# Up products of a decoder's gated MLPs: 512 columns of both activation parts at once, with the parts summed outside TensorE

## What is computed

```
def _causal_depthwise_conv(u, w, b):      # width 3, per channel
    ...
def _conv_glu_ffn(h, w_up, conv_w, conv_b, w_down):
    u = _causal_depthwise_conv(h @ w_up, conv_w, conv_b)
    gate, val = jnp.split(u, 2, axis=-1)
    return (jax.nn.silu(gate) * val) @ w_down
...
    x = x + gate2 * _conv_glu_ffn(h, ...)   # per layer
...
    return _rms_norm(x, final_gain)
```

## Time and profile before

| | us |
|---|---|
| median of 3 runs | 715.25 (714.64 to 716.34) |
| the profiled execution, its own time | 715.83 |
| span of its trace | 714.1 |
| granted TensorE clock, mean | 0.993 |
| TensorE busy | 692.5 |
| VectorE busy | 500.2 |
| ScalarE busy | 394.6 |
| GpSimd busy | 125.4 |

### The profile page before, as it was taken

The page is one execution under the profiler, slowest core; times in us unless marked ns, Lnnn a source line. Parts: engine busy times, 40 slices in busy tenths (PEclk is TensorE's granted clock), DMA queues, the critical chain, the costliest instruction groups (busy, mean ns, idle before and its releaser), DMA issues.

```text
span 714.1 us, 15023 instructions
## 1 busy us (share of the span) xinstructions
PE 692.5 (97%) x6280; PEld 649.6 (91%) x6280; DVE 500.2 (70%) x901; ACT 394.6 (55%) x633; POOL 125.4 (18%) x96
## 2 busy tenths in 40 slices
PE   7989999999999999999999999999999999999995
PEld 7787888899999999999998888879999999999993
DVE  0564897747888879798657469883786666766666
ACT  2367655734746464646545675673575555444552
POOL 2001004004054555553010010310400000000002
PEclk9999999999999999999999999999999999999998
DMA  8989987565485858587743765656536676555501
GB/s 350 382 256 302 420 297 255 185 229 178 137 314 198 296 179 295 177 293 258 292 153 128 298 246 209 215 200 237 177 117 226 130 247 226 178 177 185 189 40 59
DMA packets 76362, 159.41 MB, mean 223 GB/s; under 512 B 4071, under 2 KB 60168, under 8 KB 67592
## 3 DMA queue, kind: packets, MB, share of 16 engines
q1 hardware_dynamic: 76296, 158.46, 63.4%
HBM read 156.81 MB, written 1.64 MB: 222 GB/s over the span
## 4 chain that ended last, share of the span: by engine, by line
PE 81%; DVE 11%; ACT 4%; issue 2%; DMA 2%; SPq 0%; POOL 0%; DVEq 0%; POOLq 0%
PE bank L961 24%; PE bank L962 23%; PE bank L963 23%; PE bank L974 4%; DVE w_lo L1652 3%; DMA direct<-in_w_ada 2%; ACT work L1543 1%; DVE score L1836 1%; ACT w_hi L1403 1%; PE bank L1007 1%; DVE top L1835 1%; PE bank L1117 1%; PE bank L1222 1%; PE bank L1274 1%; DVE work L1662 1%
## 5 line engine op out<-in xcount | busy, mean ns | idle before, releaser
L961 PE MATMUL bank<-act_hi,w_hi 128*128 128x256 f32 x1040 | 298.3, 287 | 3.4 <-DVE w_lo L1652 3.3
L1652 DVE TENSOR_TENSOR w_lo<-raw,w_hi 128x2048 fp32r<-128x2048 f32 (+1 forms) x97 | 235.4, 2427 | 94.3 <-ACT w_hi L1403 94.1
L962 PE MATMUL bank<-act_lo,w_hi 128*128 128x256 f32 x1040 | 294.9, 284 | 0.0
L963 PE MATMUL bank<-act_hi,w_lo 128*128 128x256 f32 x1040 | 294.8, 283 | 0.0
L1403 ACT ACTIVATE w_hi<-raw 128x2048 fp32r<-128x2048 f32 (+1 forms) x97 | 182.9, 1888 | 140.6 <-PE bank L963 131.3
L961 PEld LDWEIGHTS bank<-act_hi,w_hi 128*128 128x128 f32 x1040 | 200.0, 192 | 7.2 <-issue 4.6
L962 PEld LDWEIGHTS bank<-act_lo,w_hi 128*128 128x128 f32 x1040 | 200.2, 192 | 0.4
L963 PEld LDWEIGHTS bank<-act_hi,w_lo 128*128 128x128 f32 x1040 | 200.1, 192 | 0.0
L1957 DVE SCALAR_TENSOR_TENSOR work<-bank,vec,work 128x254 f32<-128x254 f32 (+1 forms) x176 | 76.5, 476 | 11.1 <-ACT work L1596 9.6
L961 PE MATMUL bank<-mlp_hi,w_hi 128*128 128x256 f32 x192 | 54.7, 285 | 0.0
L962 PE MATMUL bank<-mlp_lo,w_hi 128*128 128x256 f32 x192 | 54.3, 283 | 0.0
(11 more groups left out here) (199 smaller groups left out, 913.0 us busy)
## 6 DMA issues: line engine op xcount, KB each, us to landing
direct<-in_w_ada SPq DMA_DIRECT2D x48, 1024.0 KB, 8.9
raw<-in_w_ffn_up SPq DMA_DIRECT2D x44, 1024.0 KB, 5.2
raw<-in_w_ffn_down SPq DMA_DIRECT2D x22, 1024.0 KB, 5.0
raw<-in_w_in SPq DMA_DIRECT2D x19, 1024.0 KB, 5.2
raw<-in_w_out SPq DMA_DIRECT2D x8, 1024.0 KB, 5.2
raw<-in_w_in SPq DMA_DIRECT2D x2, 984.0 KB, 11.6
bias<-toeplitz SPq DMA_DIRECT2D x4, 384.0 KB, 11.9
xT<-in_x SPq DMA_DIRECT2D x1, 1024.0 KB, 5.0
```

What stands on the lines that cost most here:

```text
L961: pe.matmul(dst, lh, rh, start=first, stop=False, skip_group_check=check)
L962: pe.matmul(dst, lh, rl, start=False, stop=False, skip_group_check=check)
L963: return pe.matmul(dst, ll, rh, start=False, stop=last, skip_group_check=check)
L1652: nc.vector.tensor_tensor(w_lo[n % RAW][:, s], raw[n % RAW][:, s], w_hi[n % RAW][:, s].bitcast(F32), ALU.subtract).then_inc(lo_done, 1)
```

## The change

Both parts of the activations lie side by side for each k (`act_both`). In steps 0 to 9 of both layers, each 128-channel tile of an up unit is now one PSUM tile of 512 columns of its own: per k one product of the high weights with both activation parts (512 columns: high x high in the left half, high x low in the right) and one of the low weights with the high part (256 columns, left half). ScalarE copies the right half to SBUF (`copy_rest`), VectorE adds the left half to it (`sum_tiles`), into `tile_sum`, and the taps read `tile_sum` instead of the bank. Step 10 is as before. The tiles take banks 0, 1, 2 in turn; in step 0 the fourth takes bank 4, in step 1 bank 7. A tile waits for the sum of the tile before it in its bank. Layer 0's last down part moves from bank 2 to bank 6. The second `take_mod` moves to step 0. The end: GpSimd multiplies with the gain only the last part, which ScalarE scales; VectorE scales the three others.

The diff, with unchanged stretches left out (the declarations of new semaphores too):

```
@@ -385,8 +385,8 @@
...
         xT = sb("xT", [P, KT, SEQ])
-        act_hi = sb("act_hi", [P, KT, SEQ], F32R)
-        act_lo = sb("act_lo", [P, KT, SEQ], F32R)
+        act_both = sb("act_both", [P, KT, 2, SEQ], F32R)
+        act_hi, act_lo = act_both[:, :, 0, :], act_both[:, :, 1, :]
         mlp_hi = sb("mlp_hi", [P, 2, SEQ], F32R)
@@ -463,7 +463,8 @@
...
         gate_row, gain_row = v_flat[:, 0:D_MODEL], v_flat[:, D_MODEL:2 * D_MODEL]
-        gained = qkT[:, 2, :, :, :].rearrange("p a b t -> p (a b t)")
+        tile_sum = qkT[:, 0, :, :, :]
+        gained = qkT[:, 2, 0, :, :].rearrange("p b t -> p (b t)")
         squared = [qkT[:, g, half, :, :].rearrange("p b t -> p (b t)") for g in (1, 3) for half in range(2)]
@@ -626,11 +630,23 @@
...
-            return bank[2][:, 0:SEQ] if ct == KT - 1 else bank[3 + ct // 2][:, (ct % 2) * SEQ:(ct % 2 + 1) * SEQ]
+            return bank[3 + ct // 2][:, (ct % 2) * SEQ:(ct % 2 + 1) * SEQ]
...
             return bank[4][:, 0:SEQ] if ct == KT - 1 else bank[ct // 2][:, (ct % 2) * SEQ:(ct % 2 + 1) * SEQ]
+
+        def tile_bank(j, which, f):
+
+            return bank[(0, 1, 2, 7 if j else 4)[2 * which + f] if j < 2 else (4 * j + 2 * which + f - 8) % 3]
+
+        def both_parts(l, j):
+
+            return j < STEPS - 1
+
+        def tiles_of(l):
+
+            return 4 * (STEPS - 1) * l
@@ -822,7 +838,7 @@
...
                 for q in range(2):
-                    sp.wait_ge(out_part[t], q + 1)
+                    sp.wait_ge(out_part[2 * t + q], 1)
                     sp.dma_start(out[0, t * P:(t + 1) * P, 512 * q:512 * q + 512],
@@ -942,15 +958,17 @@
...
                         ada_sum(e[1], e[2])
-            pool.wait_ge(gain_in, 16)
-            for q in range(2):
-                pool.wait_ge(x_out, q + 1)
-                nc.gpsimd.tensor_tensor(gained[:, 512 * q:512 * q + 512], x_tok[:, 0, 512 * q:512 * q + 512],
-                                        gain_row[:, 512 * q:512 * q + 512], ALU.mult).then_inc(row_gained, 1)
-            for t in range(TT):
+            def row_power(t):
+
                 pool.wait_ge(row_ms, t + 1)
...
                     row_root, 1)
+
+            pool.wait_ge(gain_in, 16)
+            row_power(0)
+            pool.wait_ge(x_out, 4)
+            nc.gpsimd.tensor_tensor(gained, x_tok[:, 1, 512:1024], gain_row[:, 512:1024], ALU.mult).then_inc(row_gained, 1)
+            row_power(1)
@@ -1316,15 +1334,43 @@
...
-                def up_first():
-
-                    for which, k0, k1 in [(which, k, k + 1) for k in range(KT // 2) for which in range(2)] + [
-                            (0, KT // 2, KT), (1, KT // 2, KT)]:
-                        mm = unit_product(l, NI + NO + which, bank[which], None if which else KT * (norm + 1), k0, k1)
-                        if k1 == KT:
-                            mm.then_inc(unit_used, 1)
-
-                def up(j, which):
+                def wide_tile(j, which, f, k0, k1, wait_act=None):
+
+
+                    n = unit_no(l, NI + NO + (which if j == 0 else 3 * j - 1 + which))
+                    pe.wait_ge(lo_done, n + 1)
+                    if j:
+                        tile = 4 * j + 2 * which + f
+                        pe.wait_ge(tile_summed, tiles_of(l) + (min(tile, 6) - 3 if tile < 8 else tile - (3 if tile < 11 else 2)))
+                    wh = w_hi[n % RAW][:, :].rearrange("p (k n) -> p k n", k=KT)
+                    wl = w_lo[n % RAW][:, :].rearrange("p (k n) -> p k n", k=KT)
+                    s, dst = slice(f * P, (f + 1) * P), tile_bank(j, which, f)
+                    for k in range(k0, k1):
+                        if wait_act is not None:
+                            pe.wait_ge(act_lo_ready, wait_act + k + 1)
+                        pe.matmul(dst[:, :], wh[:, k, s], act_both[:, k, :, :].rearrange("p a t -> p (a t)"),
+                                  start=k == 0, stop=False, skip_group_check=True)
+                        mm = pe.matmul(dst[:, 0:SEQ], wl[:, k, s], act_hi[:, k, :], start=False, stop=k == KT - 1,
+                                       skip_group_check=True)
+                    if k1 == KT:
+                        mm.then_inc(unit_used if f else first_tile, 1)
+
+                def wide_first():
+
+                    for k in range(KT // 2):
+                        for which in range(2):
+                            for f in range(2):
+                                wide_tile(0, which, f, k, k + 1, None if which or f else KT * (norm + 1))
+                    for which in range(2):
+                        wide_tile(0, which, 0, KT // 2, KT, None if which else KT * (norm + 1))
+                        wide_tile(0, which, 1, KT // 2, KT)
+
+                def wide_up(j, which):
+                    for f in range(2):
+                        wide_tile(j, which, f, 0, KT)
+
+                def single_up(j, which):
+                    pe.wait_ge(tile_summed, tiles_of(l) + 4 * j - 1 + which)
                     pe.wait_ge(conv_read, 2 * (STEPS * l + j - 1) + which + 1)
@@ -1343,8 +1389,8 @@
...
                             mm = product3(down_part(ct), (wh[:, f, s], wl[:, f, s]), (hi[:, f, :], lo[:, f, :]),
-                                          j == 0 and f == 0 and ct in (0, 2, 4, 6, 7), j == STEPS - 1 and f == 1, True)
-                        if j == STEPS - 1 and ct in (1, 3, 5, 6):
+                                          j == 0 and f == 0 and ct % 2 == 0, j == STEPS - 1 and f == 1, True)
+                        if j == STEPS - 1 and ct in (1, 3, 5):
                             mm.then_inc(down_ready, 1)
@@ -1378,13 +1424,17 @@
...
-                down = down_rows if l + 1 == DEPTH else down_product
-                up_first()
+                last = l + 1 == DEPTH
+                down = down_rows if last else down_product
+                wide_first()
                 for j in range(1, STEPS):
+                    up = wide_up if both_parts(l, j) else single_up
                     up(j, 0)
...
                     elif l + 1 == DEPTH and j < 6:
+                        if j == 2:
+                            pe.wait_ge(tile_summed, tiles_of(l) + 8)
                         turn_x(j - 2)
@@ -1588,19 +1638,39 @@
...
                     o = which if j == 0 else 3 * j - 1 + which
-                    act.wait_ge(unit_used, first + o + 1)
+                    if both_parts(l, j):
+                        act.wait_ge(tile_summed, tiles_of(l) + 4 * j + 2 * which + 2)
+                    else:
+                        act.wait_ge(unit_used, first + o + 1)
                     if j > 0:
...
                         ch = which * FT + 2 * j + f
-                        nc.scalar.activation(conv[:, which, f, :], bank[which][:, f * SEQ:(f + 1) * SEQ], ACT.Identity,
+                        src = tile_sum[:, which, f, :] if both_parts(l, j) else bank[which][:, f * SEQ:(f + 1) * SEQ]
+                        nc.scalar.activation(conv[:, which, f, :], src, ACT.Identity,
                                              scale=vec[:, l, V_W2 + ch:V_W2 + ch + 1],
...
+                def copy_rest(j, which):
+
+                    for f in range(2):
+                        if f:
+                            act.wait_ge(unit_used, first + (which if j == 0 else 3 * j - 1 + which) + 1)
+                        else:
+                            act.wait_ge(first_tile, tiles_of(l) // 2 + 2 * j + which + 1)
+                        nc.scalar.activation(tile_sum[:, which, f, :], tile_bank(j, which, f)[:, SEQ:2 * SEQ],
+                                             ACT.Copy).then_inc(rest_copied, 1)
+
                 for j in range(STEPS):
+                    if j and both_parts(l, j):
+                        copy_rest(j, 0)
                     if j < STEPS - 1:
                         split_hi(first + 3 * j + 2)
+                    if j == 0 and both_parts(l, j):
+                        copy_rest(j, 0)
                     last_tap(j, 0)
+                    if both_parts(l, j):
+                        copy_rest(j, 1)
                     split_hi(first + (3 * j + 3 if j < STEPS - 1 else 3 * STEPS - 1))
@@ -1629,11 +1699,9 @@
...
                                          accum_out=sums[:, t, q:q + 1]).then_inc(row_squares, 1)
-            act.wait_ge(row_root, 1)
-            for q in range(2):
-                act.wait_ge(row_gained, q + 1)
-                nc.scalar.activation(x_tok[:, 0, 512 * q:512 * q + 512], gained[:, 512 * q:512 * q + 512], ACT.Identity,
-                                     scale=root[:, 0:1]).then_inc(out_part[0], 1)
+            act.wait_ge(row_root, 2)
+            act.wait_ge(row_gained, 1)
+            nc.scalar.activation(x_tok[:, 1, 512:1024], gained, ACT.Identity, scale=root[:, 1:2]).then_inc(out_part[3], 1)
@@ -1954,8 +2022,9 @@
...
                             dst = conv[:, which, f, lag:SEQ]
```

(42 more changed lines are left out.)

5 lines of the change are left out of this document (4 added, 1 removed).

## The result

The changed kernel takes 724.65 us (median of 4 runs, 723.91 to 727.29), against 715.75 for the kernel before on the same chips. The ratio, taken over all runs and not from the two medians, is 1.0134, interval 1.0117 to 1.0152: slower by 9 us. The forecast was 713.3, and 724.65 is outside its range. The second rival named the mechanism ("the multiply gets in before the down weights' split", 719 to 723 us).

What follows compares the result with a forecast made beforehand. TensorE, busy 97% of the span, was taken to bound the kernel. Products -7.7, stalls +6.2, end -0.4 sum to -1.9 against the profiled 715.83; 713.9, less 0.6 for the runs' median, gives 713.3 us, range 706.5 to 719.5.

Steps and rivals of the forecast that it cites:

- The second rival: Layer 0: multiply gets in before the down weights' split; two such steps 719 us, four 723; chance 0.22.
- the term of +6.2 us: TensorE's stalls in layer 0, steps 2 to 9: 1.9 + 0.3 + 4.05 us, bounds 3 and 9.
- the multiply again comes just ahead of the low part: Layer 0, every second step: GpSimd's multiply holds VectorE's low part, ahead of a sum TensorE needs; multiply priced at 3.5 us.
- the formula p - 1.5: Layer 0: fourth tile's wait in us, p being the end of VectorE's product from step start; 1.9 us for step 2.
- 0.6 was forecast for an idle VectorE: Layer 0, steps 4, 6, 8: if GpSimd's later operations find VectorE idle, p falls to 2.1 and the stall to 0.6.
- the rival's 2.15: Layer 0: multiply, split, first add, low part in turn take 2.15 us more; stall 4.0 at p = 3.4.
- Three stalls were forecast at 1.35 each: Layer 0, steps 4, 6, 8: the middle between stalls of 2.0 and 0.6 us, 4.05 us together.
- Step 3's 0.3: Layer 0, step 3: 0.3 us of stall, ScalarE's scaling of 3.29 us standing before its copy of the first tile.
- the multiply and the split shift together: Layer 0: argument against the 0.20-chance rival of hidden stalls (about 708 us): VectorE's split itself issues the modulation load.
- The products: Up products, both layers: 640 pairs merged into 512 columns, 0.012 us saved each, -7.7 us, half in each layer.
- The third rival: Up products: a 256-column product after a 512-column one takes 0.132 us, merge saves nothing, about 721 us; chance 0.05.
- Taps out of SBUF: VectorE's taps reading SBUF can be held by GpSimd, delaying p; counted in the stalls' upper bound of 9.

Runs made afterwards that it cites:

- Experiment 2: Changed kernel with GpSimd's multiply and additions in layer 0's MLP cut to at most 8 columns, leaving out most of a sum: 709.82 us, ratio 0.9929.
- experiment 3: Changed kernel with GpSimd's multiply in layer 0 waiting for VectorE's low part of the step before: 716.7 us, ratio 1.0024.
- Experiment 4: Changed kernel with VectorE's sum of the next step's first tile queued ahead of the low part: 717.87 us, ratio 1.0026.
- experiment 6: Changed kernel with the first tile's sum ahead of the low part and its copy ahead of ScalarE's scaling: 722.72 us; also with low products last: 722.17.
- the best version: Changed kernel with the new products in layer 1 alone, low products behind the wide ones in each tile: 710.93 us, ratio 0.9945.
- experiment 7: Changed kernel with GpSimd's multiply behind the low part, first tile's sum and copy first: 717.73 us; also with low products last: 716.9.
- Experiment 10: Kernel before the change with the new end alone: 715.6 us, ratio 0.9994.
- experiment 8: Changed kernel with low products behind the wide ones in each tile (first kernel): 723.95 us; with each wide product split into two of 256 columns: 726.73.

## Why the prediction was wrong

**What failed is the price of the waits**, the term of +6.2 us: 10.6 was measured, and some 5 us more for TensorE's clock behind them, which no term had. The place, the releaser and the kind were right: the fourth tile of steps 2, 4, 6 and 8 waits for VectorE's sum, and layer 1 has no waits. The step that failed is "the multiply again comes just ahead of the low part", taken for all four steps. It holds for two of them, and there the formula p - 1.5 is good. In step 2 the fourth tile was due at 212.18, so the step began 3 x 2.82 earlier at 203.7, the product ended at 206.7, p is 3.0 and the formula gives 1.5 against 1.35. In step 6, 0.6 was forecast for an idle VectorE, and 0.53 came. In steps 4 and 8 the multiply started ahead of the split or of the product. For step 4, p is 3.5: the formula says 2.0, and the rival's 2.15 on top makes 4.2 against 4.03. Step 8 is worse by a case that I hadn't listed: the product itself is held. Three stalls were forecast at 1.35 each; they were 4.03, 0.53 and 4.66. Step 3's 0.3 did not appear.

I had argued that the multiply and the split shift together because VectorE releases the load. The trace shows the multiply 0.04 us ahead of the split in step 4 and 0.07 us ahead of the product in step 8, and the multiply is released by the landing of a load, 8.0 us behind its issue in step 4 (235.02). Where two starts are that close, with 2 us at stake each, a chance of 0.22 for the bad side was too low. Experiment 2 shows the cause by taking GpSimd's long operations out, and experiment 3 by fixing the order: both lose all waits of the even steps. Experiment 4 shows the part of the low part, for steps where the multiply comes inside the split; where it comes before the product, the sum's place doesn't help (5.5 and 4.3 us in experiment 6).

**The clock was missing.** No term and no rival had TensorE's clock fall behind a long wait. In this profile it is 5 us, half as much as the waits. With the products' smaller gain (3.3 us less than forecast, below) it is why the second rival's own price, 723 us for four such steps, was reached with two. The whole difference between the forecast for the profiled execution (-1.9) and its span (+11.5) is 13.4 us: waits 4.4, clock about 5, products 3.3 and the end 0.2 make 12.9.

**The products were over-priced:** -7.7 forecast, -4.4 measured. From 269.46 to 275.11 there are 16 pairs, 0.353 us each instead of 0.348 (3 x 0.120 before, so 0.007 saved). Both kinds of product kept their price only next to their own kind: with the low products last a tile takes 2.79 us in the changed kernel and 2.76 in the best version, 0.349 and 0.345 a pair. Alternating costs some 0.005 us a pair, which no row of the kernel before could show, as it had no alternation. The third rival had the direction, with more than twice the size.
The figure of 2.5 ns of fixed cost is what the Trainium skill, TensorE: Matmul & The Clock Gate, section "Back-to-back issue gap", gives for a matmul by itself, and it says there that the figure falls short for narrow ones in a stream with weight loads. By it 640 pairs would have saved 1.6 us, an estimate; the low-last tiles saved more, 0.360 less 0.349 to 0.345, which makes 7.0 to 9.6.

**Taps out of SBUF:** named as part of the upper bound. That they can be held was right: they took 3.31 us for four in steps 2 and 3 and up to 8.7 in the variants, where those out of PSUM keep 1.77 beside a busy GpSimd. This agrees with the lock between VectorE and GpSimd of the Trainium skill, SBUF — State Buffer, section "SBUF: two separate sides". In the changed kernel the four taps right ahead of the product kept 1.78 to 1.79 us in each of the steps 2, 4, 6 and 8, so they don't show in its waits directly. I take them for what left experiment 7 with no room; no kernel with its orders and taps out of PSUM was run.

**Layer 1 and the end:** no waits, as forecast. Layer 1 gained 2.3 us, 0.007 for each of its 320 pairs, where half of -7.7 was forecast, and the end 0.2 where 0.4 was. Experiment 10 puts it at nothing measurable.

**Open.** The clock's part isn't measured by itself, only read from windows. And why two of the four steps fall on the bad side of the race was seen in the traces of single executions; how often each side comes up over many executions wasn't tried. The trace of experiment 8's first kernel has the multiply ahead in the same two steps, by 0.25 and 0.12 us, with waits of 4.08 and 4.66, so it need not be chance.

## What to carry to other kernels

Before TensorE is made to wait for an operation on another engine, list what is queued ahead of that operation, and for each item which engine can hold it; where two starts are within a few tenths of a microsecond, price both orders and call neither unlikely. A change that pays only in TensorE's stream (here 0.3 to 0.6% of the time) should go first where GpSimd is silent. An idle stretch of TensorE of several microseconds is to be priced with the slow stretch behind it.

## What the runs showed of the hardware

- In these traces, which of two engines holds the other is settled by which starts first. A multiply of GpSimd 0.04 us ahead of VectorE's split made it 5.73 us; one 1.6 us behind its start left it at 2.29 (steps 4 and 2). Where both have work queued, their operations went in turn: product 4.11, split 4.49.
- TensorE's granted clock fell to 1.2 GHz in waits of 4.03 and 4.66 us, and behind one of 3.0 us though 1.9 us of work stood in front of it; there it fell only after TensorE had resumed. In the kernel with copy and sum first and the low products last it fell behind a wait of 2.53 us, and not behind one of 2.66. In the kernel of experiment 3 with the scaling moved it fell behind a wait of 2.15 us at layer 0's end, with eight products of one column in front of it. Behind waits for a sum of up to 1.9 us no fall was seen. So the length of a wait alone doesn't tell.
- A matmul of 512 columns takes 0.228 us next to its kind; in turn with one of 256 the two take 0.353 instead of 0.345 to 0.349.
